# First modulations in two feature halves, and the first mixer's products in whole fp32

## The chip, the cores and the metric

The kernel runs on one core of one Trainium2 chip. The metric is the time on the device for one execution, in microseconds (us), as the median of several runs. TensorE (PE) does the matrix products, VectorE (DVE) and ScalarE (ACT) the elementwise work, GpSimd (POOL) issues some DMAs and does a little elementwise work, SyncE (SP) only issues DMAs. The engines run side by side and wait for each other on semaphores; each of them takes its own instructions strictly in the order of the program.

## The reference, cut to what matters

The input is x, 256 tokens of 1024 features, and a vector c. There are two layers of one model and two of a second one. All of it is fp32. What the change touches is the opening of the first layer:

```
c_act = silu(c)
mod   = (c_act @ mod_w[0] + mod_b[0])      # 1024 x 6144; six vectors of 1024
hin   = x * (1 + mod[1]) + mod[0]          # scale and shift, from the first 2048 columns
# first mixer (mla)
proj  = hin @ w_in                         # 1024 x (256 + 256 + 64): q rank, kv rank, rotary key
c_q   = rms_norm(proj[:, :256], q_norm);   c_kv = rms_norm(proj[:, 256:512], kv_norm)
k_r   = rope(proj[:, 512:])
q     = c_q @ w_uq                         # 256 x (8 heads x (128 + 64)), the 64 rotated
kv    = c_kv @ w_ukv                       # 256 x (8 heads x (128 + 128))
o     = causal softmax attention;  y = o @ w_o
x     = layer_norm(alpha * x + mod[2] * y);  then a gated convolutional ffn, and so on
```

## The kernel before, in words

The kernel is one hand-written program for each engine. Activations are kept transposed, features on the 128 partitions and the 256 tokens along the free dimension ("tiles(t, a, b)" is columns a*256 to b*256, one tile for 128 features).

**Weights.** All weight matrices come through one ordered list of chunks (weight_stream), each of up to 1 MB in two units. SP issues their DMAs into a ring of RAW = 3 chunks called raw. For each unit ACT writes a rounded copy to w_hi (L1058, in fp32r, the one-pass format of TensorE) and DVE the remainder, raw minus w_hi, to w_lo (L1575). Activations are split in the same way (h_hi and h_lo, o_hi and o_lo). A product is then three matmuls, hi x hi, lo x hi and hi x lo (L529 to L531 with the features as output, L535 to L537 with the tokens). ACT and DVE split AHEAD = 5 units in front of the product; "ahead(u)" issues the splits up to unit u and "product(key)" does this and then waits for the product's last matmul. SP refills a slot of raw when both units in it have been split.

**Modulations.** The vectors mod are sums over 8 row blocks of 128 rows (k = 0 to 7). They are not done on TensorE: for each row block, 128 x 2048 numbers are brought in, DVE multiplies them by c_act's column and adds them to modsum (L1602 for the first, L1605 for the others; this is modulate(count)). After eight of them, TensorE transposes modsum in blocks of 128 and DVE reduces over the columns (fold: L601 and L1623); coefficients() then writes scale and shift to lncol. Group 0 is the 2048 columns that hin needs; the 80 further row blocks of groups 1 to 10 are summed by DVE in gaps all through the program, fed by POOL's DMAs through the two slots of modraw, each refilled when the block two before has been summed. Of group 0 two blocks come through POOL into modraw, four through SP's queue (n in early, into the raw ring and into vv), two more through POOL.

**Opening, in order.** SP: c, the identity, the positions (broadcast, and once in a form of 4-byte pieces), the other constants, four blocks of group 0, x, small vectors, then the weights, of which the first three chunks (mla_in) wait until DVE has read the blocks of modulation in their slots. ACT: silu, then 17 DMAs of small parameter vectors into prow, which TensorE transposes (L783) and ACT copies to cols. TensorE: c, the parameters, x (L790), a small product for the relative bias (L796), the fold of group 0, then mla_in chunks 0, 1, 2. DVE: the eight sums of group 0 with the rotary angles between them, the fold, then for each of the 8 feature tiles hf (L1651) and h_lo (L1658), with ACT's h_hi (L1068). From mla_in the ranks go through squares, a sum by a matmul with ones (L813), a square root on ACT (L1311), reciprocal and scaling on DVE (L1955, L1958), a split into o_hi and o_lo (L1315, L1963); then uq(0), swap(0), ukv(0), uq(1), score of the first head and the attention loop, in which TensorE does ukv(1) at steps 0 and 1 and the first units of mla_o from step 4. DVE's part of a step begins with L1824 and ends with one modulate. Eight sums of groups 1 and 2 each: six are made before the attention loop, ten in it.

Of the kernel before, what the change touches and what calls it, by code (L numbers as in the profile page):

```python
# [16 lines left out]
P = 128  # L17
D = 1024
# [95 lines left out]
def weight_stream(w):  # L114
# [21 lines left out]
    cols(("mla_in", 0), mla_in, 0)  # L136
    cols(("mla_in", 1), mla_in, 256)
    cols(("mla_in", 2), mla_in, 512, 64)
# [43 lines left out]
def modulation_stream(w):  # L182
# [16 lines left out]
    for g in range(len(groups)):  # L199
        rows(g, groups[g])  # L200
    return out


def build(nc, w, consts, out):
# [5 lines left out]
    mods = modulation_stream(w)  # L210
# [8 lines left out]
    for n, (key, parts, _) in enumerate(chunks):  # L219
        count[n % RAW] += 16 * {"uq": 2, "wax": 1}.get(key[0], len(parts))  # L220
        landed.append(count[n % RAW])


    early = range(MODRAW, MODRAW + RAW + 1)
# [9 lines left out]
    with ExitStack() as ctx:  # L234
# [76 lines left out]
        ranks = kk[:, 8 * S:12 * S]  # L311
# [3 lines left out]
        mod_width = [max(sum(src.shape[1] for src, _ in parts) for h, _, parts in mods if h == g) for g in range(NG)]  # L315
# [49 lines left out]
        def unit_ap(ring, u):  # L365
            n = u // 2
            half_len = length[n] // 2
            return ring[:, (u % UNITS) * UL:(u % UNITS) * UL + half_len]
# [9 lines left out]
        def raw_unit(u):  # L378
            n = u // 2
            half_len = length[n] // 2  # L380
            return raw[:, n % RAW, (u % 2) * half_len:(u % 2 + 1) * half_len]
# [13 lines left out]

        beside_units = {
            "mla": {t: unit0("ukv", 1) + t for t in range(2)} | {t: unit0("mla_o", 0) + t - 4 for t in range(4, 9)},
# [9 lines left out]

        def early_slot(n):
            return raw[:, n - MODRAW, :] if n < MODRAW + RAW else vv[:, 0:2048]
# [5 lines left out]
        def _(sp):  # L415
            for i, name in enumerate(("c", "c_2")):
                sp.dma_start(prow[8 * i:8 * i + 8, 0:P],
                             w[name].rearrange("a (n q) -> (a n) q", q=P)).then_inc(sem("c_in"), 16)
            sp.dma_start(cst[:, C_ID:C_ID + P], consts[:, C_ID:C_ID + P]).then_inc(sem("ident_in"), 16)
            sp.dma_start(pos_i, w["positions"].broadcast_to([P, S])).then_inc(sem("pos_in"), 16)  # L420
            sp.dma_start(posq_i[:, :], w["positions"][0].rearrange("(t p) -> p t", p=P), allow_slow_non_contiguous=True).then_inc(sem("pos_in"), 16)
# [1136 lines left out]
        def _(dve):  # L1558
# [381 lines left out]
            for m in range(KT + 1):  # L1940
# [3 lines left out]
                if m:  # L1944
                    h_low(0, m - 1)
# [330 lines left out]
```

## Time and profile before

| | |
|---|---|
| median of 3 runs | 941.89 us (940.87 to 942.15) |
| the profiled execution | 945.47 us, span 943.7 us from the first to the last instruction |
| PE busy | 844.6 us, 90% of the span |
| DVE busy | 739.3 us, 78% |
| ACT busy | 526.4 us, 56% |
| DMA | 216.31 MB, mean 229 GB/s |
| first three-matmul product begins | 49.4 us into the span |
| first row maximum of the first attention (L1824) | 102.1 us |

[...]

### The profile page before, as it was taken

To read this page: it belongs to the slowest core of one execution; us is meant where nothing else is said; L and a number is where in the kernel's file an instruction comes from. 1 tells how busy PE (TensorE), PEld (TensorE's weight loads), DVE (VectorE), ACT (ScalarE), POOL (GpSimd) and SP (SyncE) were. 2 spreads that over 40 slices of the span, in tenths; PEclk is the share of its full clock that TensorE was granted. 3 is DMA by queue.
4 is the path that set the end of the run, shared out by engine and by line. 5 is a ranking of instruction groups with operands and counts; after the bars stand their busy time and mean duration, and the time that the engine had idled before them with its cause. 6 is when DMAs were issued, how large, how long until landed. Compare 5 with 4: busy or idle time off the path is not lost.

```text
span 943.7 us, 14975 instructions
## 1 busy us (share of the span) xinstructions
PE 844.6 (90%) x5749; PEld 776.7 (82%) x5749; DVE 739.3 (78%) x1153; ACT 526.4 (56%) x899; POOL 80.8 (9%) x118
## 2 busy tenths in 40 slices
PE   0386798999999998999999999999788999999886
PEld 0376677999999998999789999999677899879874
DVE  2879878878788778889878888676768866788886
ACT  0354665654444447449584345544474768766783
POOL 1000010002000000014000022010000000000120
PEclk9887989999999999999999999999989999999989
DMA  8966746577978864995956789987444784437431
GB/s 324 311 217 204 289 159 203 186 273 240 345 273 296 299 217 147 382 371 176 350 172 225 282 262 289 270 237 248 155 123 125 245 276 171 150 121 244 135 134 44
DMA packets 122678, 216.31 MB, mean 229 GB/s; under 512 B 12235, under 2 KB 97975, under 8 KB 115440
## 3 DMA queue, kind: packets, MB, share of 16 engines
q1 hardware_dynamic: 106828, 134.79, 42.9%
q0 software_dynamic: 12960, 72.46, 22.1%
q10 hardware_dynamic: 2820, 8.11, 2.6%
q8 instruction: 46, 0.75, 0.3%
q14 instruction: 24, 0.20, 0.1%
HBM read 214.18 MB, written 1.15 MB: 228 GB/s over the span
## 4 chain that ended last, share of the span: by engine, by line
PE 60%; DVE 21%; ACT 9%; DMA 5%; issue 4%; SPq 0%; DVEq 0%; ACTq 0%
PE bank L529 11%; PE bank L530 11%; PE bank L531 11%; PE bank L535 7%; PE bank L537 7%; PE bank L536 7%; DVE w_lo L1575 4%; DVE modsum L1605 3%; DMA raw<-in_mod_w 2%; DMA modraw<-in_mod_w 2%; ACT w_hi L1058 1%; ACT kk L1125 1%; PE bank L601 1%; PE bank L596 1%; PE bank L655 1%
## 5 line engine op out<-in xcount | busy, mean ns | idle before, releaser
L529 PE MATMUL bank<-h_hi,w_hi 128*128 128x256 f32 (+2 forms) x1184 | 341.7, 289 | 19.9 <-DVE h_lo L1728 9.2
L1575 DVE TENSOR_TENSOR w_lo<-raw,w_hi 128x1024 fp32r<-128x1024 f32 (+2 forms) x250 | 291.8, 1204 | 67.4 <-ACT w_hi L1058 66.9
L530 PE MATMUL bank<-h_lo,w_hi 128*128 128x256 f32 (+2 forms) x1184 | 337.3, 285 | 0.0
L531 PE MATMUL bank<-h_hi,w_lo 128*128 128x256 f32 (+2 forms) x1184 | 337.2, 285 | 0.0
L1058 ACT ACTIVATE w_hi<-raw 128x1024 fp32r<-128x1024 f32 (+2 forms) x250 | 249.2, 1028 | 81.3 <-PE bank L531 28.2
L529 PEld LDWEIGHTS bank<-h_hi,w_hi 128*128 128x128 f32 (+2 forms) x1184 | 228.3, 193 | 26.2 <-issue 21.5
L530 PEld LDWEIGHTS bank<-h_lo,w_hi 128*128 128x128 f32 (+2 forms) x1184 | 228.5, 193 | 1.4 <-issue 0.5
L531 PEld LDWEIGHTS bank<-h_hi,w_lo 128*128 128x128 f32 (+2 forms) x1184 | 228.2, 193 | 0.2
L535 PE MATMUL bank<-w_hi,o_hi 128*128 128x512 f32 x312 | 124.9, 400 | 0.6 <-issue 0.6
L537 PE MATMUL bank<-w_hi,o_lo 128*128 128x512 f32 x312 | 121.7, 390 | 0.0
L536 PE MATMUL bank<-w_lo,o_hi 128*128 128x512 f32 x312 | 121.7, 390 | 0.0
L1605 DVE SCALAR_TENSOR_TENSOR modsum<-modraw,small,modsum 128x2048 f32<-128x2048 f32 (+1 forms) x45 | 90.7, 2015 | 6.7 <-DMA modraw<-in_mod_w 4.1
L535 PEld LDWEIGHTS bank<-w_hi,o_hi 128*128 128x128 f32 x312 | 58.7, 188 | 13.4 <-issue 2.2
L537 PEld LDWEIGHTS bank<-w_hi,o_lo 128*128 128x128 f32 x312 | 58.6, 188 | 12.7
L536 PEld LDWEIGHTS bank<-w_lo,o_hi 128*128 128x128 f32 x312 | 58.8, 188 | 11.4 <-issue 0.5
L471 POOL DMA_DIRECT2D modraw<-in_mod_w x52 | 27.9, 536 | 382.3 <-DVE modsum L1605 134.0
L1250 ACT ACTIVATE kk<-kk 128x512 f32<-128x512 f32 x22 | 13.9, 632 | 72.3 <-DVE kk L1876 72.3
L471 POOL DMA_DIRECT2D modraw<-in_ada_w x32 | 17.4, 545 | 382.9 <-DVE modsum L1605 199.0
L1605 DVE SCALAR_TENSOR_TENSOR of<-modraw,small,of 128x2048 f32<-128x2048 f32 (+1 forms) x21 | 41.9, 1995 | 3.5 <-DMA modraw<-in_mod_w 1.2
L1256 ACT ACTIVATE o_hi<-kk 128x512 fp32r<-128x512 f32 x22 | 13.9, 632 | 45.9 <-DVE kk L1880 43.9
L1245 ACT ACTIVATE kk<-bank,cols 128x256 f32<-128x256 f32 x44 | 22.4, 559 | 28.8 <-PE bank L531 28.5
L608 PE MATMUL bank<-h_hi,o_hi 128*128 128x256 f32 x141 | 22.2, 309 | 7.0 <-DVE prob L1677 3.8
(274 smaller groups left out, 1151.5 us busy)
## 6 DMA issues: line engine op xcount, KB each, us to landing
raw<-in_ffn_w_in SPq DMA_DIRECT2D x88, 512.0 KB, 6.0
modraw<-in_mod_w POOLq DMA_DIRECT2D x36, 1024.0 KB, 6.4
raw<-in_ffn_w_out SPq DMA_DIRECT2D x44, 512.0 KB, 7.2
modraw<-in_ada_w POOLq DMA_DIRECT2D x16, 1024.0 KB, 5.4
raw<-in_attn_w_in SPq DMA_DIRECT2D x26, 512.0 KB, 5.3
raw<-in_moba_w_in SPq DMA_DIRECT2D x24, 512.0 KB, 8.6
modraw<-in_mod_w POOLq DMA_DIRECT2D x16, 512.0 KB, 4.7
modraw<-in_ada_w POOLq DMA_DIRECT2D x16, 512.0 KB, 4.8
```

What stands on the lines that cost most here:

```text
L471: pool.dma_start(modraw[:, slot, at:at + src.shape[1]], src).then_inc(sem(f"mod_in{slot}"), 16)
L529: pe.matmul(dst, cut(hi(u)), a_hi, start=first, stop=False, skip_group_check=True)
L530: pe.matmul(dst, cut(hi(u)), a_lo, start=False, stop=False, skip_group_check=True)
L531: return pe.matmul(dst, cut(lo(u)), a_hi, start=False, stop=last, skip_group_check=True)
L535: pe.matmul(dst, a_hi, cut(hi(u)), start=first, stop=False, skip_group_check=True)
L536: pe.matmul(dst, a_hi, cut(lo(u)), start=False, stop=False, skip_group_check=True)
L537: return pe.matmul(dst, a_lo, cut(hi(u)), start=False, stop=last, skip_group_check=True)
L608: pe.matmul(bank[0][:, 0:S], o_hi[:, 0:P], tiles(h_hi, 0, 1), start=True, stop=True, skip_group_check=True)
L1058: act.activation(hi(v), raw_unit(v), ACT.Copy).then_inc(sem("w_hi_ready"), 1)
L1245: act.activation(tiles(conv, s, s + 1), bank[0][:, t * S:(t + 1) * S], ACT.Identity, bias=cb[:, f:f + 1], scale=w2[:, 2 * FT + f:2 * FT + ...
L1575: dve.tensor_tensor(lo(v), raw_unit(v), hi(v).bitcast(F32), ALU.subtract).then_inc(sem("w_lo_ready"), 1)
L1605: ins = dve.scalar_tensor_tensor(acc, src, ck, acc, ALU.mult, ALU.add)
```

## The change

Five things are changed together.

1. Group 0 is summed in two feature halves. first_half[k] holds, of shift and scale, the features 0 to 511 of row block k (128 x 2 x 512 numbers in pieces of 2 KB); the other half is the new group 0 of the list. The first halves are brought in first, the even ones by SP and the odd ones by POOL (x goes between k = 1 and k = 3 on POOL), and summed, folded and used for four feature tiles before DVE sums the second halves. ACT alone writes hf (first_rows); h_hi and h_lo of this norm are gone.
2. The chunks of mla_in are cut differently: (q, kv) of rows 0 to 511, (rotary of rows 0 to 511, q of rows 512 to 1023), (rotary and kv of rows 512 to 1023), so that three units need only the first four feature tiles.
3. mla_in, uq and ukv are multiplied in whole fp32 directly from raw: one matmul in place of three. Their 14 units are not split by ACT and DVE any more (both begin at split0, the first unit of mla_o), and SP refills their slots when TensorE has used them (w_used). The ranks stay fp32, in vv, and are not split.
4. The splits of mla_o fall into the attention loop, one unit a step.
5. The order of the DMAs: positions, the columns of constants and the buckets go behind mla_in, the other constants behind two more chunks; ACT issues mod_b and the three blocks of PB[2] first. The cosine's angle is derived from the sine's.

```diff
+    by_half = mod[0].rearrange("(k p) c -> k p c", p=P)[:, :, 0:2048].rearrange("k p (n h c) -> k p n h c", n=2, h=2)
+            for k in (0, 2, 4, 6):
+                first_modulation(k)
+            weights(0)
+            weights(1, (0,))
+            for n in (0, 2, 4, 6):
+                sp.wait_ge(sem("first_summed"), max(n - 1, 5))
+                sp.dma_start(row_halves(early_slot(n)), mods[n][2][0][0]).then_inc(sem(f"mod_early{n}"), 16)
+            weights(1, (1,))
+            weights(2)
...
+                if 2 * (n - RAW) < split0:
+                    sp.wait_ge(sem("w_used"), 2 * (n - RAW) + 2)
+                else:
+                    sp.wait_ge(sem("w_lo_ready"), 2 * (n - RAW) + 2 - split0)
...
+            for k in (1, 3, 5, 7):
+                if k == 3:
+                    pool.dma_start(x[:, :].rearrange("p (t f) -> p t f", t=2),
+                                   w["x"][0].rearrange("(t p) f -> p t f", p=P)).then_inc(sem("x_in"), 16)
+                pool.dma_start(row_halves(first_slot(k)), first_half[k]).then_inc(sem(f"first_in{k}"), 16)
...
+            mla_unit(0, bank[0], 0)
+            mla_unit(1, bank[1], 0)
+            mla_unit(2, bank[2], 0, 64)
+            pe.wait_ge(sem("x_copied"), 4)
+            fold(0, (4, 5), (1, 3))
...
+            mla_unit(3, bank[0], 1)
+            mla_unit(4, bank[2], 1, 64)
+            pe.wait_ge(sem("bias_row"), 1)
+            rank_sum(0)
+            mla_unit(5, bank[1], 1)
+            rank_sum(1)
...
+                    for i in range(6):
+                        ins = pe.matmul(bank[5 + i // 2][:, (i % 2) * S:(i % 2 + 1) * S],
+                                        raw_unit(u)[:, i * P:(i + 1) * P], ranks[kt], start=kt == 0 and i % 2 == 0,
+                                        stop=kt == 1, skip_group_check=True)
...
             uq(0)
+            ukv_unit(0, 0)
             swap(0)
-            ukv_unit(0, 0)
             ukv_unit(0, 1)
             uq(1)
...
+            first_rows(0)
+            first_rows(1)
...
-            ahead(AHEAD)
-            for m in range(KT):
-                act.wait_ge(sem("h_full"), m + 1)
-                h_high(0, m, qz)
...
+            for k in range(KT):
+                acc, src = of_half(modsum[:, :], 0), row_halves(first_slot(k))
+                dve.wait_ge(sem(f"first_in{k}"), 16)
...
+            first_coefficients(0)
+            modulate(KT)
+            first_coefficients(1)
+            dve.wait_ge(sem("columns_in"), 16)
+            angles()
...
+            modulate(1)
+            rank_normed(0)
+            modulate(1)
+            rank_normed(1)
...
+            rotate(0)
+            modulate(3)
...
-            "mla": {t: unit0("ukv", 1) + t for t in range(2)} | {t: unit0("mla_o", 0) + t - 4 for t in range(4, 9)},
+            "mla": {t: split0 + t + 1 - AHEAD for t in range(-1, 9)},
```

## Rows read from the trace of the kernel before

**Rows 1.** Page, chain that ended last: shares by engine.

```profile
PE 60%; DVE 21%; ACT 9%; DMA 5%; issue 4%; SPq 0%; DVEq 0%; ACTq 0%
```

**Rows 2.** Busy time by stretch: PE, PEld, DVE, ACT, POOL, clock, DMA share, GB/s.

```profile
0.00:10.00 10.00, 0.28 (x1) 0.18 (x1) 1.41 (x3) 1.47 (x2) 2.74 (x9) 1.00 0.62 222
10.00:20.00 10.00, 0.00 (x0) 0.00 (x0) 4.19 (x2) 0.00 (x0) 0.53 (x1) 1.00 1.04 395
40.00:45.00 5.00, 3.79 (x16) 3.00 (x16) 3.13 (x4) 1.10 (x3) 0.53 (x1) 0.50 0.94 347
45.00:50.00 5.00, 0.65 (x4) 0.63 (x4) 4.25 (x11) 1.48 (x3) 0.00 (x0) 0.84 0.18 72
50.00:55.00 5.00, 4.86 (x23) 4.57 (x22) 4.53 (x12) 3.21 (x6) 0.00 (x0) 0.50 0.07 29
...
0.00:34.00 34.00, 3.72 (x17) 3.37 (x18) 16.95 (x21) 3.27 (x9) 3.27 (x10) 1.00 0.91 341
34.00:102.00 68.00, 49.69 (x303) 44.67 (x301) 57.59 (x76) 34.23 (x51) 4.30 (x8) 0.82 0.69 233
```

**Rows 3.** Timeline of 0 to 50 us: DVE's last sums, TensorE's fold, first product.

```profile
36.25 4.81 DVE L1605 SCALAR_TENSOR_TENSOR modsum<-modraw,small,modsum 128x2048 f32<-128x2048 f32 x2
41.21 3.84 PE L601 MATMUL bank<-cst,modsum 128*128 128x128 f32 x16 [5.13 <-DVE modsum L1605]
46.23 0.17 DVE L1645 COPY lncol<-modc 128x8 f32<-128x8 f32 x1
49.40 0.55 PE L529 MATMUL bank<-h_hi,w_hi 128*128 128x256 f32 x1 [4.35 <-DVE h_lo L1658]
```

**Rows 4.** Groups by line and form, 0 to 103 us: busy, mean ns, idle before.

```profile
L1575 DVE TENSOR_TENSOR w_lo<-raw,w_hi 128x1024 fp32r<-128x1024 f32 x11 | 13.1, 1220 | 1.1 <-ACT w_hi L1058 0.9
L1058 ACT ACTIVATE w_hi<-raw 128x1024 fp32r<-128x1024 f32 x11 | 11.2, 1056 | 5.9 <-PE bank L537 3.2 <-PE bank L531 2.2 <-DMA raw<-in_mla_w_ukv 0.5
L1068 ACT ACTIVATE h_hi<-qz,lncol 128x256 fp32r<-128x256 f32 x8 | 4.7, 598 | 8.1 <-DVE kk L1651 7.9
L1955 DVE RECIPROCAL rstd<-rstd 128x256 f32<-128x256 f32 x2 | 3.5, 1750 | 1.0 <-ACT rstd L1311 1.0
L1623 DVE TENSOR_REDUCE modc<-bank 128x4 f32<-128x512 f32 x4 | 2.8, 692 | 2.0 <-PE bank L601 2.0
L1958 DVE SCALAR_TENSOR_TENSOR kk<-bank,cols,rstd 128x256 f32<-128x256 f32 x4 | 1.8, 481 | 0.1
```

**Rows 5.** The same view, 102 to 150 us: sums over 1024 columns.

```profile
L1605 DVE SCALAR_TENSOR_TENSOR kk<-modraw,small,kk 128x1024 f32<-128x1024 f32 x7 | 9.0, 1280 | 4.3 <-DMA modraw<-in_mod_w 4.3
L1602 DVE TENSOR_SCALAR kk<-modraw,small 128x1024 f32<-128x1024 f32 x1 | 0.7, 745 | 0.0
```

**Rows 6.** Timeline of PE: spacing of split products, whole products, transposes.

```profile
51.25 0.41 PE L531 MATMUL bank<-h_hi,w_lo 128*128 128x256 f32 x1
51.46 0.41 PE L529 MATMUL bank<-h_hi,w_hi 128*128 128x256 f32 x1
...
57.12 0.28 PE L529 MATMUL bank<-h_hi,w_hi 128*128 128x256 f32 x1
57.24 0.28 PE L530 MATMUL bank<-h_lo,w_hi 128*128 128x256 f32 x1
...
97.31 0.59 PE L655 MATMUL bank<-of 128*128 128x256 f32 x2
97.75 0.38 PE L652 MATMUL bank<-kk,qz 128*128 128x128 f32 x2
```

**Rows 7.** Waits of 0 to 150 us, and DMA issues with median time to landing.

```profile
PE bank L783 <- DMA kk<-in_ffn_conv_b: 25.1, 1, 25.1
...
modraw<-in_mod_w POOLq DMA_DIRECT2D x12, 1024.0 KB, 5.9
```

**Rows 8.** Timeline of DVE about the first attention's start.

```profile
102.11 0.28 DVE L1824 CUSTOM_DVE_ANT_0 prob<-bank,cst 128x128 f32<-128x128 f32 x1
```

More of the change, by code:

```diff
@@ L209, in build @@
     length = [k * width for k, (_, _, width) in zip(row_tiles, chunks)]
-    mods = modulation_stream(w)
+    unit_len = [n // 2 for n in length for _ in range(2)]
+    paired = ("mla_in", "wax")
+    for n, (key, parts, _) in enumerate(chunks):
+        if key[0] in paired:
+            unit_len[2 * n:2 * n + 2] = [src.shape[1] * src.shape[2] for src, _ in parts]
+    mods, first_half = modulation_stream(w)
     NG = 1 + max(g for g, _, _ in mods)
@@ L219, in build @@
     for n, (key, parts, _) in enumerate(chunks):
-        count[n % RAW] += 16 * {"uq": 2, "wax": 1}.get(key[0], len(parts))
+        count[n % RAW] += 16 * {"uq": 2, "wax": 1, "mla_in": 1}.get(key[0], len(parts))
         landed.append(count[n % RAW])
-    early = range(MODRAW, MODRAW + RAW + 1)
+    early = range(KT)
     mod_slot = [n % MODRAW for n in range(len(mods))]
@@ L450, in _ @@
+            for i in range(2):
+                sp.dma_start(bf[8 * i:8 * i + 8, :], w["attn_b_f_2"].rearrange("a b -> b a"), allow_slow_non_contiguous=True).then_inc(
+                    sem("attn_in"), 16)
+            for n in range(RAW + 2, len(chunks)):
+                free_chunk(n)
+                weights(n)
             for t in range(2):
@@ L466, in modulation @@
                     slot = mod_slot[n]
[L467 to L469 removed]
+                    pool.wait_ge(sem("mod_summed"), {KT: 6, KT + 1: 8}.get(n, n - MODRAW + 1))
                     for src, at in mods[n][2]:
@@ L1283, in _ @@
                     at += n
+            for m in range(4):
+                act.wait_ge(sem("x_turned"), 2 * m + 2)
+                act.activation(tiles(qz, 2 * m, 2 * m + 2), bank[4 + m][:, :], ACT.Copy).then_inc(sem("x_copied"), 1)
             act.wait_ge(sem("params_turned"), 1)
@@ L1931, in _, with rank_normed @@
             link(dve.tensor_scalar(angle, pos, const(C_COL), None, ALU.mult))
-            modulate(1)
-            angles(sin, 0.0)
-            modulate(2)
-            angles(cos, 0.25)
-            modulate(2)
-            fold(0, (2, 0))
-            coefficients(0, mod8(0, 0), mod8(0, 1))
-            ahead(0)
-            for m in range(KT + 1):
-                if m < KT:
-                    dve.wait_ge(sem("x_copied"), m // 2 + 1)
-                    h_full(0, m, tiles(qz, m, m + 1))
-                if m:
-                    h_low(0, m - 1)
-            product("mla_in", 0)
-            modulate(1)
-            product("mla_in", 1)
-            for j in range(2):
-                if j:
-                    product("mla_in", 2)
+            angles()
+            def rank_normed(j):
                 dve.wait_ge(sem("c_rooted"), j + 1)
@@ L1982, in rotate @@
                                   ALU.add).then_inc(sem("q_rotated"), 1)
-            product("uq", 0)
             modulate(1)
-            rotate(0)
-            modulate(1)
-            product("ukv", 0)
+            dve.wait_ge(sem("const_in"), 16)
             causal = lambda t: (mask[:, 0:P], mask[:, P:CAUSAL])
```

317 lines of the change are left out of this document (170 added, 147 removed).

## The prediction

> **What bounds the kernel now.** I read the chain that ended last first: TensorE holds 60% of it, DVE 21%, DMA only 5% [rows 1]. So the kernel is TensorE-bound on the whole, but not in its opening. The busy times by stretch show that: up to 34 us TensorE works 3.7 us, up to 102 us another 50 of 68 [rows 2]. Before 34 us the DMA runs at 341 GB/s, after that at 233 [rows 2]. The timeline then gives the order of the opening: the eighth sum of group 0 ends at 41.06, the fold's transposes run 41.21 to 45.05, the coefficients are there at 46.4, the first product starts at 49.40 [rows 3], and the first attention's row maximum is at 102.11 [rows 8]. What follows 102 us is, but for small things, the same program in both kernels. So I work out when the changed kernel reaches that row maximum, and take what it gains there as the gain of the whole.
>
> **Step 1, first halves.** DMA has to bring 4 MB of first halves, 1 MB of x and 0.3 MB of the rest, and half of the 1.1 MB of weights behind the halves on SP gets in between: 5.85 MB. By 10 us 2.2 MB have moved (222 GB/s), then 0.395 MB a us [rows 2]: all is there at 10 + 3.65 / 0.395 = 19 us. A sum over 1024 columns is 1.28 us, the first of a group 0.75 [rows 5]; DVE needs 9.7 us for the eight and keeps up. They end at 20.3. A whole half-size pipeline could be as early as 18 or, if small pieces cost rate, 23. The parameters must be there too: now TensorE waits 25.1 us for the last of them [rows 7], to 29.4. I read that as small packets that take turns with 8 KB ones; against 2 KB ones they should be done by about 15. That is the least certain cover, and a rival below.
>
> **Step 2, to the first product.** Now 5.3 us pass from the last sum to the coefficients, with 16 transposes in 3.84 [rows 3]. Eight take 1.9, then one reduce of 0.69 [rows 4] and three small steps of 0.2: 3.4 us, so 23.7. One tile of hf on ACT is 0.6 (as the h_hi tile [rows 4]): TensorE starts at 24.3, not 49.4.
>
> **Step 3, whole products.** Split products of 256 columns start 0.21 us apart at the low clock and 0.12 at the high one; a whole product (two records) starts 0.43 before the next matmul at the high clock (97.31 to 97.75) [rows 6], so 0.86 at the low one. Three split ones are 0.36, so whole is dearer by 0.07 each. There are 40 in mla_in, 24 in uq, 32 equivalents in ukv: 96 x 0.07 = 7 us more of TensorE. Against that fall 14 units of splits, 1.22 us each at full width on DVE and 1.06 on ACT [rows 4], some 14 and 12 us with the shorter ones, all of which stand before the row maximum. [...]
>
> TensorE has been idle, so it starts low: at 49.4 it needed some 5 us before the spacing fell (clock 0.50 in 50 to 55 [rows 2]). First three units, 20 products: 6 at 0.86, 14 at 0.43, 11.2 us, to 35.5. Beside them DVE sums the second halves: 9.7 us from 23.7, to 33.4; their 4 MB (and rest of the weights) are there at 19 + 4.5 / 0.4 = 30.5, so DMA is hidden by 1.6 us. Second fold: eight transposes 1.0 at the high clock (half of the low price), reduce 0.7, small steps 0.9: 38.1, and hf on ACT to 38.7. Here TensorE is idle for some 2 us. If the clock falls there, the next 5 us run at half, 2.5 us lost. [...]
>
> **Step 4, ranks.** Units 3 and 4, 12 products: 5.2, to 43.9; sum with ones 0.86; unit 5, 3.4, to 48.2; square 0.6 and sum 0.9: 49.7. Root 0.4, reciprocal 1.75, two scalings of 0.48 [rows 4]: 52.8, then the rotary key's five small steps, 2.1: 54.9. The roots, reciprocals and angles for q are hidden under unit 5. TensorE's kr_spread waits for the constants, which now stand behind two chunks on SP; these go out after unit 3 (about 42), so they land near 51. uq(0) from 51.5, 12 x 0.43 = 5.2, to 56.7; ukv unit 0 (8 equivalents, 3.4) to 60.1; swap 0.9 to 61.0. Up to 1.3 us of constants are in this; each us later is a us on the path.
>
> **Step 5, DVE up to attention.** rotate(0), three passes of 0.7, to 63.1; then modulate(3), 2.4 each (two in 4.81 [rows 3]). The first two end at 67.9. The third waits: its slot of modraw is free when the first of them is summed (65.5), and landing takes 5.9 [rows 7], so 71.4, summed at 73.8. TensorE is done with the second ukv unit at 64.4 and with uq(1) at 69.6, and has scores at 71; it does not set the time. Row maximum at 73.8 instead of 102.1: 28.3 us earlier. Check by bytes: up to 102 us 34 x 0.341 + 68 x 0.233 = 27.4 MB moved [rows 2]; without the 2 MB of mla_o that may come later, 25.4 must be there by 71.4, a mean of 0.38 after the first 10 us, just under the 0.395 seen. So DMA is nearly the bound there; it can cost more, hardly give more.
>
> **Step 6, in attention.** DVE gets two more splits in the loop, ACT three (2.4 and 3.2 us, over ten steps), ukv(1) is 1.3 us longer, and TensorE no longer runs ahead of DVE at its start. What hides it: DVE's waits for modraw (4.3 us in this stretch [rows 5]) and ACT's slack. Nothing excludes that all 2.4 of DVE's splits show, nor that none does; I take 1.3. Everything later, the 64 sums of the later groups and all splits after mla_o's, is unchanged.
>
> **Sum.** 28.3 - 1.3 = 27 us. The span of 943.7 becomes 916.7, the profiled execution of 945.5 becomes 918.5. The median is 3.6 below that execution, 941.9: forecast 915.
>
> **Rivals.**
> - *The first half isn't early.* Parameters or first halves come as late as the parameters do now, 29.4 [rows 7]. The DMA share is 1.04 from 10 us on [rows 2], so they do compete; for me speaks that they are issued earlier and against smaller packets. 9 us of the 27 go: 924. Chance 14%.
> - *DMA paces the way to attention.* If it moves 0.35 MB a us instead of 0.395 after 10 us (pieces of 1 KB, slots freed late, a queue behind), 25.4 MB take until 76.3, and the two-slot stream then stays behind through its ten sums, some 4 more: 922. For it: the narrow byte check. Against: the sums in the loop have slack. 14%.
> - *Slower: TensorE stays at the low clock with whole products.* From 24.3: 17.2, fold and hf 4, then 10.3, 1.7, 6.9, 2.3, 1.7, uq 10.3, ukv 6.9, swap 1.7, 6.9, uq(1) 10.3, scores 2.6: 107 instead of 102, and ukv(1) of 13.8 us, where TensorE now runs ahead, 5 more: 952. It decides as soon as a whole product costs 0.8 us on average on this path. Against it: whole products of attention are at 0.43 [rows 6], and dense work always brought the high clock. 4%.
> - *More than forecast.* Halves at 17 us, no clock loss, TensorE ready first: 5 to 7 us more, 909. 8%.
> - *Forecast*, 915, with 910 to 920 as its own range: 60%.
>
> **How the numbers follow.** From no change to this kernel's measurement uncertainty is 0.2%, 1.9 us. All cases but one are faster; faster 0.94, same 0.02 (mixtures of the low clock and late data), slower 0.04. The range takes in both late cases and the early one: 907 to 926.
>
> **What would show it.** Right: first product near 24, the second stretch of products near 39, spacing 0.43 a product for most of them, uq starting before 53, row maximum of the first head at 74, then an attention loop of some 48 to 50 us as now, and the rest shifted. Wrong: a wait of TensorE for parameters after 20 us, long waits for modraw or raw between 50 and 80, a clock of 0.50 over several stretches, or the gain at the row maximum being lost again before the first layer norm.

## The result, and the profile after

The changed kernel takes 929.61 us (median of 4 runs, 928.32 to 931.48) against 941.68 (4 runs of the kernel before on the same chip): ratio 0.9864, 95% interval 0.983 to 0.9898. It is 12.1 us faster; 27 were forecast, and 929.6 lies above the range of 907 to 926. The profiled execution took 929.42, its span is 927.6.

The chain that ended last, shares by engine, answers to [rows 1]; then the busy time by stretch, columns as in [rows 2]:

```profile
PE 62%; DVE 17%; ACT 10%; DMA 6%; issue 4%; POOL 0%; DVEq 0%; ACTq 0%; POOLq 0%
```

```profile
0.00:10.00 10.00, 0.28 (x1) 0.18 (x1) 2.16 (x4) 1.67 (x3) 4.76 (x11) 1.00 0.76 253
10.00:20.00 10.00, 4.65 (x21) 4.09 (x21) 5.77 (x5) 2.39 (x4) 0.74 (x1) 1.00 1.05 376
...
40.00:45.00 5.00, 3.79 (x10) 3.08 (x11) 4.50 (x15) 4.04 (x7) 0.18 (x1) 0.66 1.14 354
...
50.00:55.00 5.00, 4.10 (x18) 2.96 (x16) 4.86 (x4) 0.97 (x3) 0.00 (x0) 1.00 0.95 339
...
0.00:34.00 34.00, 14.82 (x55) 12.35 (x56) 17.99 (x21) 6.96 (x16) 7.66 (x15) 1.00 0.97 338
34.00:102.00 68.00, 56.89 (x228) 41.80 (x227) 45.42 (x76) 25.02 (x52) 6.41 (x11) 0.91 0.80 269
```

VectorE's share of the chain fell from 21% to 17%, and TensorE now works 14.8 us of the first 34 instead of 3.7. But the clock is 0.66 from 40 to 45 us, and it falls once more, to 0.84 and then to 0.50 over a whole stretch:

```profile
55.00:60.00 5.00, 1.79 (x5) 0.98 (x5) 2.63 (x3) 2.31 (x4) 0.53 (x1) 0.84 1.02 317
60.00:65.00 5.00, 5.00 (x13) 4.01 (x13) 4.67 (x8) 0.00 (x0) 0.17 (x1) 0.50 0.63 233
```

At the start of this trace the clock column does not show how fast TensorE is: it reads 1.00 for the first 34 us, though the first 20 products take 11.45 us below and would take 8.6 at 0.43 each. There the spacing of starts is to be read, not the column.

The timeline of the kernel after, in order of time (start, length, engine, line); its rows answer to [rows 3] and [rows 8]:

```profile
19.37 2.67 DVE L1995 SCALAR_TENSOR_TENSOR modsum<-of,small,modsum 128x1024 f32<-128x1024 f32 x2 [1.04 <-DMA of<-in_mod_w]
...
26.19 11.45 PE L855 MATMUL bank<-kk,raw 128*128 128x256 f32 x40 [2.12 <-ACT kk L1362]
...
28.44 2.67 DVE L1678 SCALAR_TENSOR_TENSOR modsum<-modraw,small,modsum 128x1024 f32<-128x1024 f32 x2 [0.91 <-DMA modraw<-in_mod_w]
32.27 2.67 DVE L1678 SCALAR_TENSOR_TENSOR modsum<-modraw,small,modsum 128x1024 f32<-128x1024 f32 x2 [1.15 <-DMA modraw<-in_mod_w]
...
37.86 1.07 PE L651 MATMUL bank<-cst,modsum 128*128 128x128 f32 x8 [0.23 <-DVE modsum L1678]
...
41.21 7.25 PE L855 MATMUL bank<-kk,raw 128*128 128x256 f32 x24 [1.33 <-ACT kk L1362]
...
47.84 0.71 SPq L483 DMA_DIRECT2D cst<-in_constants  x1
...
53.66 1.13 PE L865 MATMUL bank<-kk,ones 128*128 128x256 f32 x4 [0.69 <-ACT kk L1374]
58.21 1.84 PE L892 MATMUL bank<-kk,cst 64*128 64x256 f32 x4 [3.42 <-issue]
59.98 8.04 PE L905 MATMUL bank<-vv,raw 128*128 128x256 f32 x24
...
72.36 0.69 DVE L2051 TENSOR_TENSOR kk<-of,bias 128x512 f32<-128x512 f32 x1 [5.79 <-PE bank L916]
...
74.42 4.81 DVE L1678 SCALAR_TENSOR_TENSOR modsum<-modraw,small,modsum 128x2048 f32<-128x2048 f32 x2
...
75.60 5.34 PE L905 MATMUL bank<-vv,raw 128*128 128x256 f32 x24
...
84.78 2.35 DVE L1678 SCALAR_TENSOR_TENSOR modsum<-modraw,small,modsum 128x2048 f32<-128x2048 f32 x1 [5.55 <-DMA modraw<-in_mod_w]
...
87.05 0.29 DVE L1886 CUSTOM_DVE_ANT_0 prob<-bank,cst 128x128 f32<-128x128 f32 x1
```

The reader is to see three things. (A whole product is two records, 40 for the 20 of the first three units, where each of the split ones in [rows 6] is one; L855 is mla_in, L892 kr_spread, the small product for the rotary key, and L905 uq. The durations recorded there overlap, 0.28 us with starts 0.12 apart, so a product's price is the spacing of starts.) The row maximum of the first head comes at 87.05, not at 73.8. The same 24 records (12 products) of L905 take 8.04 us at 59.98 and 5.34 at 75.60: that is the clock, 0.50 from 60 to 65 us and 1.00 from 75 to 80. And two gaps grew: 3.42 us before kr_spread (L892), which the view puts down to "issue", and 5.55 us of VectorE before its last sum. From the row maximum to the end it is 840.5 us, 841.6 before: what was gained stands at this point. The program has two waits before kr_spread, for the fold and for the constants, and the word "issue" names neither. The constants were issued at 47.84 and took 10.3 us to land, to 58.14, just before the 58.21; e1 below tests it.

Against the prediction's own steps, in us:

| step | forecast | after | late by | new at this step |
|---|---|---|---|---|
| first product | 24.3 | 26.19 | 1.9 | 1.9 |
| its 20 products end | 35.5 | 37.6 | 2.1 | 0.2 |
| second stretch of products | 38.7 | 41.2 | 2.5 | 0.4 |
| units 3 and 4 end | 43.9 | 48.4 | 4.5 | 2.0 |
| second sum with ones ends | 49.7 | 54.8 | 5.1 | 0.6 |
| uq(0) starts | 51.5 | 60.0 | 8.5 | 3.4 |
| uq(0) ends | 56.7 | 68.0 | 11.3 | 2.8 |
| rotate(0) ends | 63.1 | 74.4 | 11.3 | 0 |
| row maximum | 73.8 | 87.05 | 13.2 | 1.9 |

### The profile page after: what moved, and what is told of

Same layout as the page of the kernel before. It is cut to its first block, busy times and chain, and to the rows that moved or that the text cites. A ratio compares the mean times of both kernels' runs of the same rounds, so it can differ in the third digit from the quotient of the medians.

```text
span 927.6 us, 14747 instructions
## 1 busy us (share of the span) xinstructions
PE 854.4 (92%) x5661; PEld 777.5 (84%) x5661; DVE 718.8 (77%) x1124; ACT 514.1 (55%) x885; POOL 85.7 (9%) x123
## 3 DMA queue, kind: packets, MB, share of 16 engines
HBM read 214.18 MB, written 1.15 MB: 232 GB/s over the span
## 4 chain that ended last, share of the span: by engine, by line
PE 62%; DVE 17%; ACT 10%; DMA 6%; issue 4%; POOL 0%; DVEq 0%; ACTq 0%; POOLq 0%
PE bank L579 11%; PE bank L580 11%; PE bank L581 11%; PE bank L585 7%; PE bank L587 7%; PE bank L586 7%; DMA modraw<-in_mod_w 6%; DVE w_lo L1646 3%; DVE modsum L1678 3%; ACT w_hi L1127 2%; ACT kk L1189 1%; PE bank L705 1%; PE bank L855 1%; DVE kk L2238 1%; DVE x L1743 1%
## 5 line engine op out<-in xcount | busy, mean ns | idle before, releaser
L579 PE MATMUL bank<-h_hi,w_hi 128*128 128x256 f32 x1144 | 330.3, 289 | 15.6 <-DVE h_lo L1790 9.2
L1646 DVE TENSOR_TENSOR w_lo<-raw,w_hi 128x1024 fp32r<-128x1024 f32 (+1 forms) x236 | 278.1, 1215 | 64.2 <-ACT w_hi L1127 63.8
L580 PE MATMUL bank<-h_lo,w_hi 128*128 128x256 f32 x1144 | 326.2, 285 | 0.0
L581 PE MATMUL bank<-h_hi,w_lo 128*128 128x256 f32 x1144 | 326.0, 285 | 0.0
L1127 ACT ACTIVATE w_hi<-raw 128x1024 fp32r<-128x1024 f32 (+1 forms) x236 | 238.1, 1036 | 75.1 <-PE bank L581 29.2
L579 PEld LDWEIGHTS bank<-h_hi,w_hi 128*128 128x128 f32 x1144 | 220.9, 193 | 21.0 <-issue 15.2
L580 PEld LDWEIGHTS bank<-h_lo,w_hi 128*128 128x128 f32 x1144 | 221.1, 193 | 1.5 <-issue 0.5
L581 PEld LDWEIGHTS bank<-h_hi,w_lo 128*128 128x128 f32 x1144 | 220.8, 193 | 0.4
L585 PE MATMUL bank<-w_hi,o_hi 128*128 128x512 f32 x304 | 121.7, 400 | 1.5 <-DVE o_lo L2179 0.8
L585 PEld LDWEIGHTS bank<-w_hi,o_hi 128*128 128x128 f32 x304 | 57.2, 188 | 14.3 <-issue 3.3
L586 PEld LDWEIGHTS bank<-w_lo,o_hi 128*128 128x128 f32 x304 | 57.2, 188 | 11.3 <-issue 0.5
L1945 DVE TENSOR_TENSOR o_lo<-kk,o_hi 128x512 fp32r<-128x512 f32 x22 | 15.2, 692 | 16.7 <-ACT o_hi L1320 16.7
```

The source lines that it names most:

```text
L579: pe.matmul(dst, cut(hi(u)), a_hi, start=first, stop=False, skip_group_check=True)
L580: pe.matmul(dst, cut(hi(u)), a_lo, start=False, stop=False, skip_group_check=True)
L581: return pe.matmul(dst, cut(lo(u)), a_hi, start=False, stop=last, skip_group_check=True)
L585: pe.matmul(dst, a_hi, cut(hi(u)), start=first, stop=False, skip_group_check=True)
L586: pe.matmul(dst, a_hi, cut(lo(u)), start=False, stop=False, skip_group_check=True)
L1127: act.activation(hi(v), raw_unit(v), ACT.Copy).then_inc(sem("w_hi_ready"), 1)
```

## The experiments

The theory that I set out to test: three costs, in series, make the 13 us. The constants that kr_spread needs are issued behind two weight chunks; the clock falls in each gap of TensorE; and the two-slot stream of modulation rows has its sums in the wrong places, three of them in a row just ahead of the attention. All kernels below are the kernel after with the edit shown; "row maximum" is that of the first head in the profiled execution (one for each kernel, two for after and before). The runs stood on several chips, on which the median of the kernel before was 941.5 to 943.4 us; the ratio is taken on the same chip, so two medians of the table that lie 1 or 2 us apart are not told apart by them.

| run | median us | ratio to before, 95% | row maximum |
|---|---|---|---|
| after (again, e11) | 929.16 | 0.9864 (0.9842 to 0.9886) | 86.90 |
| e1 constants early | 924.61 | 0.9805 (0.9776 to 0.9833) | 79.41 |
| e2 sums forward | 928.02 | 0.9843 (0.9818 to 0.9868) | 85.93 |
| e3 both | 919.40 | 0.9754 (0.9726 to 0.9782) | 76.58 |
| e4 filler | 924.80 | 0.9804 (0.9777 to 0.9832) | 81.73 |
| e5 one stage | 934.18 | 0.9901 (0.9882 to 0.992) | 91.18 |
| e6 order2 | 918.40 | 0.9744 (0.9721 to 0.9767) | 75.31 |
| e7 order2, filler | 918.26 | 0.9726 (0.9703 to 0.975) | 74.24 |
| e8 x last | 927.39 | 0.9834 (0.9811 to 0.9858) | 86.01 |
| e9 weights held | 917.70 | 0.9742 (0.9719 to 0.9765) | 74.87 |
| e10 order2, one stage | 927.85 | 0.984 (0.9815 to 0.9865) | 84.32 |
| e13 halves on POOL | 916.74 | 0.972 (0.9696 to 0.9745) | 74.10 |

**e1.** The transfer of the constants is moved:

```diff
             sp.dma_start(prob[0:BUCKETS + 1, 0:2 * S],
                          consts[0:BUCKETS + 1, C_BUCKET:C_END]).then_inc(sem("buckets_in"), 16)
+            sp.dma_start(cst[:, P:C_COL], consts[:, P:C_COL]).then_inc(sem("const_in"), 16)
...
             for n in (RAW, RAW + 1):
                 free_chunk(n)
                 weights(n)
-            sp.dma_start(cst[:, P:C_COL], consts[:, P:C_COL]).then_inc(sem("const_in"), 16)
```

> The constants of the rotary key and the mask are issued on SP before the fourth weight chunk (near 34 us) instead of behind the fifth (47.8). Theory A (the wait for them and the low clock behind it cost the row maximum some 7 us): TensorE starts kr_spread near 55 instead of 58.2, at the high clock, uq(0) takes 5.2 to 5.5 us instead of 8.0, the row maximum of the first head comes at about 80 instead of 87.05, the median is 922 to 924. Theory B (the two-slot stream of modulation rows paces the opening, so that a faster TensorE only makes VectorE wait longer): uq(0) is as fast as in A, but the row maximum comes at 85 or later and the median is 927 or more. Theory C (data: an early transfer of 0.45 MB pushes the weights or second halves back): a new wait of 1 to 2 us ahead of 45 us and a median of 929 or more.

Measured 924.61, 5.0 us less than the kernel after. Its timeline:

```profile
26.31 10.58 PE L855 MATMUL bank<-kk,raw 128*128 128x256 f32 x40 [2.11 <-ACT kk L1362]
...
41.41 5.56 PE L855 MATMUL bank<-kk,raw 128*128 128x256 f32 x24 [1.32 <-ACT kk L1362]
...
53.23 1.13 PE L892 MATMUL bank<-kk,cst 64*128 64x256 f32 x4
54.29 5.45 PE L905 MATMUL bank<-vv,raw 128*128 128x256 f32 x24
...
77.14 2.35 DVE L1678 SCALAR_TENSOR_TENSOR modsum<-modraw,small,modsum 128x2048 f32<-128x2048 f32 x1 [5.16 <-DMA modraw<-in_mod_w]
79.41 0.28 DVE L1886 CUSTOM_DVE_ANT_0 prob<-bank,cst 128x128 f32<-128x128 f32 x1
```

The gap named "issue" is gone, so it was the wait for the constants, and uq(0) runs at the high clock (5.45 us, 1.00 in the column from 50 to 60). Of the 7.6 us at the row maximum 1.7 are not the edit's: units 3 and 4 took 5.56 us here, but 7.25 in e3 and e6, which have the same edit, and this execution (921.11) is the fastest of its five. The wait of 5.16 us for the stream stays. Theory A, with the median 0.6 above its range; B and C fall.

**e2.** Only the order of VectorE's sums of group 1:

```diff
-            modulate(1)
+            modulate(2)
             rank_normed(0)
             modulate(1)
             rank_normed(1)
...
             modulate(1)
             dve.wait_ge(sem("const_in"), 16)
...
+            modulate(1)
             rotate(0)
-            modulate(3)
+            modulate(1)
```

> The six sums of the second group that stand before the attention are moved on VectorE, nothing else: two instead of one before the first rank scaling, then one, then one behind the rotary key, one between distances and rotate(0), one behind it, instead of 1, 1, 1 and three behind rotate(0). They use the 4.2 us idle ahead of 50 us, the 2.5 ahead of 52.6 and the 5.8 ahead of rotate(0). Theory A (TensorE with its wait and clock sets rotate(0) at 72.4, the stream only the 5.5 us of wait behind it and two sums of 2.4): the row maximum comes as soon as scores are there, 81 to 82 instead of 87.05, median 924 to 925.5. Theory B (the stream alone is what is late): the same 5 us here, but then e1 brings nothing. Theory C (what is gained ahead of the attention is lost in it, because ring and slots are no further): row maximum at 82 and a median above 928.

Measured 928.02, 1.6 us less than the kernel after, whose runs it overlaps; 924 to 925.5 was expected. The theory was incomplete, and the timeline says why:

```profile
48.45 0.53 POOL L510 DMA_DIRECT2D modraw<-in_mod_w  x1 [2.33 <-DVE modsum L1678]
...
61.73 2.04 PE L892 MATMUL bank<-kk,cst 64*128 64x256 f32 x4 [7.42 <-issue]
...
78.06 2.35 DVE L1678 SCALAR_TENSOR_TENSOR modsum<-modraw,small,modsum 128x2048 f32<-128x2048 f32 x1
85.93 0.29 DVE L1886 CUSTOM_DVE_ANT_0 prob<-bank,cst 128x128 f32<-128x128 f32 x1 [5.53 <-PE bank L705]
```

The wait of VectorE for the stream ahead of its last sum is gone as foreseen. But a slot that is free earlier starts a transfer of 1 MB earlier (48.45; 55.19 in the kernel after), beside the constants. These take 14.3 us to land instead of 10.3, and kr_spread starts 3.5 us later still. The row maximum now waits for TensorE's scores. An earlier transfer took its time from the one that mattered.

**e3.** Both edits.

> e1 and e2 together. If TensorE's wait and clock and the stream of modulation rows are two costs in series, as theory A has it, they add up: row maximum of the first head at 74 to 77, median 916 to 920. If both only hide one another (theory B), the better of the two remains: row maximum at 80 or later, 922 or more.

Measured 919.40 and 76.58: theory A. Together they bring 10.2 us, apart 5.0 and 1.6, so that they do more than add up: e2 alone delays the constants, and e1 alone leaves the wait for the stream.

**e4.** Products that nobody reads, in TensorE's two gaps:

```diff
+            def filler(count, b):
+                for _ in range(count):
+                    pe.matmul(bank[b][:, 0:S], ones[:, :], tiles(hf, 0, 1), start=True, stop=True,
+                              skip_group_check=True)
...
+            filler(4, 6)
             mla_unit(3, bank[0], 1)
...
+            filler(8, 5)
             pe.wait_ge(sem("fold_summed"), 2)
             pe.wait_ge(sem("const_in"), 16)
```

> The kernel after with TensorE kept at work in its two gaps by products whose result nobody reads: four (1.7 us) after the second fold, eight (3.4 us) before the wait for the constants. Constants and order of sums are as in the kernel after, so that only the clock changes. Theory A (the low clock after each gap costs 2.0 and 3.8 us): units 3 and 4 take 5.3 us instead of 7.25, uq(0) 5.3 instead of 8.04, rotate(0) starts near 68.5 instead of 72.4, the row maximum is 3 to 4 us earlier and the median 925.5 to 927. If the clock falls whatever TensorE does there (power or another cause): spacing of 0.86 us stays, and the median is 929 or a little more by the fillers themselves.

Measured 924.80: 4.8 us for 5.6 us of useless work, and 0.7 more than the best that was expected. Its timeline:

```profile
25.95 11.59 PE L855 MATMUL bank<-kk,raw 128*128 128x256 f32 x40 [2.12 <-ACT kk L1369]
...
41.41 5.49 PE L855 MATMUL bank<-kk,raw 128*128 128x256 f32 x24
...
57.98 5.45 PE L912 MATMUL bank<-vv,raw 128*128 128x256 f32 x24
```

Every stretch from 40 to 80 us shows a clock of 1.00, and rotate(0) starts at 67.78. No other instruction was moved, so the low clock costs some 5 us, with the later constants that follow from it: 4.8 in the median, 5.3 at the row maximum (81.73).

**e5.** Second fold ahead of the first product:

```diff
+            pe.wait_ge(sem("x_copied"), 4)
+            fold(0, (4, 5), (1, 3))
             mla_unit(0, bank[0], 0)
             mla_unit(1, bank[1], 0)
             mla_unit(2, bank[2], 0, 64)
-            pe.wait_ge(sem("x_copied"), 4)
-            fold(0, (4, 5), (1, 3))
```

> The kernel after with the second fold put ahead of the first three product units on TensorE: the products start only when all sums are there, as if the group had one stage; whole products, transfers and the order of sums stay. Theory A (halves are worth the work that TensorE does before the second fold, 11.5 us less the two gaps with low clock): second fold near 37.3, first product near 39.5 instead of 26.2, 32 products in a row to 57, unit 4 done 8 to 9 us later than the 48.46 of the kernel after, the wait for the constants gone, row maximum at 93 to 96, median 935 to 938. Rival (the halves are worth nothing, what was gained came from whole products and from the order of the transfers alone; what follows is paced by the stream): row maximum at 87 to 89 and a median of 930 to 931.

Measured 934.18 and 91.18, both just under the ranges of theory A. The timeline of this kernel:

```profile
39.49 10.07 PE L855 MATMUL bank<-kk,raw 128*128 128x256 f32 x40
...
50.44 5.59 PE L855 MATMUL bank<-kk,raw 128*128 128x256 f32 x24
...
64.11 1.10 PE L892 MATMUL bank<-kk,cst 64*128 64x256 f32 x4 [1.74 <-issue]
65.13 7.13 PE L905 MATMUL bank<-vv,raw 128*128 128x256 f32 x24
```

TensorE starts 13.3 us later than in the kernel after and has lost only 4.1 by the row maximum: no gap after the fold, half of the wait for the constants, one low stretch fewer. So in the kernel after the halves are worth 3 to 4.6 us: 4.6 by the medians (934.2 less 929.6), 4.1 at the row maximum, and 2.9 if each gain is taken against the kernel before on its own chip (12.1 and 9.2). The other parts of the change, which e5 keeps, make the rest of the 12.1, some 7.5 to 9; how it divides between whole products and the order of transfers was not tried.

**e6.** As e3, third sum behind the rotary key:

```diff
-            modulate(1)
+            modulate(2)
             rank_normed(0)
-            modulate(1)
             rank_normed(1)
...
-            modulate(1)
+            modulate(2)
             dve.wait_ge(sem("const_in"), 16)
...
             rotate(0)
-            modulate(3)
+            modulate(2)
```

> As e3, but the third sum of the second group stands behind the rotary key instead of before the second rank scaling, since in e3 VectorE waited 2.7 us for its row there and held back the rotary key, for which TensorE then waited 1.24. Theory A: rotary key ready near 58 instead of 61.9, no wait of TensorE ahead of ukv, row maximum at 75.3 instead of 76.6, median 917.5 to 919.5. Rival: the stream is a sum behind again and the last sum before the attention ends at 78 or later; median 920 or more.

Measured 918.40 and 75.31, 1.3 earlier than e3 at the row maximum; the wait before ukv is gone. Theory A; in the medians 1.0 is within the runs' spread.

**e7.** e6 with `filler(4, 6)` as in e4.

> e6 with four products that nobody reads (1.7 us) in the gap after the second fold, as in e4. Theory A (the low clock after this gap of 1.3 to 1.5 us costs 1.7 us in units 3 and 4, whatever else is mended): these units take 5.5 us instead of 7.25, row maximum near 73.6, the time of the prediction, and a median of 915 to 917.5. Rival: with TensorE earlier, the rows of group 1 or the constants are late instead: the gain at unit 4 is 1.7 us, at the row maximum below 0.5, and the median that of e6.

```profile
37.72 1.06 PE L651 MATMUL bank<-cst,modsum 128*128 128x128 f32 x8 [0.86 <-DVE modsum L1684]
...
39.66 1.99 PE L871 MATMUL bank<-kk,ones 128*128 128x256 f32 x8
41.49 5.49 PE L855 MATMUL bank<-kk,raw 128*128 128x256 f32 x24
...
54.30 5.45 PE L911 MATMUL bank<-vv,raw 128*128 128x256 f32 x24
...
71.97 2.35 DVE L1684 SCALAR_TENSOR_TENSOR modsum<-modraw,small,modsum 128x2048 f32<-128x2048 f32 x1 [1.25 <-DMA modraw<-in_mod_w]
74.24 0.28 DVE L1892 CUSTOM_DVE_ANT_0 prob<-bank,cst 128x128 f32<-128x128 f32 x1
```

Row maximum 74.24, 0.4 from the forecast's 73.8. Of the 1.3 us that uq(0) starts earlier than in e6, 1.1 are left at the row maximum, since the stream now ends last again (1.25 at 71.97), and none is seen in the median, 918.26. Between the two readings written down beforehand: the short units are A's, the time is the rival's. That the filler made the units short is not shown here: the first three units took 10.80 us, and in e1 and e8, where they took 10.58 and 10.70, units 3 and 4 were short without any filler. Only e4, with 11.59, shows the filler at work.

**e10.** e6 with the second fold first, as in e5: what are the halves worth once the wait for the constants and the order of the sums are mended?

> As e6 with the second fold ahead of the first product, as in e5. Theory A (half of the worth of the halves was given back to the two gaps with low clock and to the wait for the constants, which one stage does not have): against e7 (no gap, constants early) the one stage now costs what it costs at unit 4, 55.97 less 46.91, some 9 us: row maximum at 82.5 to 84, median 926 to 928. Rival (the halves are worth 4 to 5 us, whatever stands behind them, since the stream or the data sets the row maximum): row maximum at 78 to 80, median 922 to 923.

Measured 927.85 and 84.32: 9.6 us slower than e7, 10.1 at the row maximum, and 10.2 slower than e9 below, which ran on the same chip. Theory A. The halves are worth some 10 us here, of which the kernel as changed kept 3 to 4.6.

**e8.** x behind all first halves on POOL.

```diff
             for k in (1, 3, 5, 7):
-                if k == 3:
-                    pool.dma_start(x[:, :].rearrange("p (t f) -> p t f", t=2),
-                                   w["x"][0].rearrange("(t p) f -> p t f", p=P)).then_inc(sem("x_in"), 16)
                 pool.dma_start(row_halves(first_slot(k)), first_half[k]).then_inc(sem(f"first_in{k}"), 16)
+            pool.dma_start(x[:, :].rearrange("p (t f) -> p t f", t=2),
+                           w["x"][0].rearrange("(t p) f -> p t f", p=P)).then_inc(sem("x_in"), 16)
```

> The kernel after with the 1 MB of x issued behind all first halves on POOL instead of behind the first of them. Theory A (the eight first sums wait 4.3 us for halves because 7 MB share the first 20 us): sums end at 19.5 to 20.3 instead of 22.04 and, if x is there by 15, the first product starts near 24.3 as predicted instead of 26.2; median at most 1 to 2 us better. Rival (x is then the late one: it lands near 19, its sixteen transposes of 3.7 us and the parameters' stand before the fold): sums at 20, but the first product at 27 to 28, median 930 to 931.

**e9.** e7 with the first weights held back on SP.

```diff
-            weights(0)
-            weights(1, (0,))
+            sp.wait_ge(sem("first_summed"), 3)
+            weights(0, (0,))
             for n in (0, 2, 4, 6):
...
-            weights(1, (1,))
+            weights(0, (1,))
+            weights(1)
             weights(2)
```

> As e7, but SP issues the first 0.5 MB of weights only after three first halves are summed and the next 0.5 MB behind the second halves, so that the first halves share the first 20 us with 0.7 MB less. Theory A (first halves are late by their share of the transfers, but TensorE and VectorE then meet a data bound on all of the first 38 us): the eight first sums end near 20.3 instead of 22, the first product starts near 24.5, and the second sums still end at 36.5 to 38; row maximum within 1 us of e7's 74.2, median 917 to 919.5. Rival (the 1.9 us late start is on the path): row maximum 1.5 to 2 us earlier, median 915 to 916.5. Second rival: the weights of unit 0 or 1 are now late, TensorE waits for them, median 920 or more.

**e13.** e7 with the first halves 1 to 6 on POOL, and 0, x and 7 on SP.

```diff
-            for k in (0, 2, 4, 6):
-                first_modulation(k)
+            first_modulation(0)
+            sp.dma_start(x[:, :].rearrange("p (t f) -> p t f", t=2),
+                         w["x"][0].rearrange("(t p) f -> p t f", p=P)).then_inc(sem("x_in"), 16)
+            first_modulation(7)
...
-            for k in (1, 3, 5, 7):
-                if k == 3:
...
+            for k in range(1, 7):
```

> As e7, but six of the eight first halves are issued on POOL and only the first and the last, with x between them, on SP (in e7 POOL has four and x, SP four). e8 and e9 showed that neither x nor the weights hold back the eighth sum: SP's fourth half landed 15.7 to 15.9 us after its issue in all three, while SP's queue moved 0.13 MB a us and POOL's 0.25. Theory A (the queue with a third of the rate has half of the data): by these rates POOL's six halves are there at 17.5, SP's share at 18.1, the eight sums end near 20.2 instead of 22.0, the first product starts near 24.3, the prediction's figure; at the row maximum 1 to 2 us earlier than e7's 74.2, unless the 12.5 MB of the first 38 us bound the second sums. Median 916 to 918.5. Rival (the total rate of some 0.38 MB a us alone sets the last landing, whatever queue): sums end at 21.5 to 22.2, first product at 25.8 or later, nothing changes.

These three ask why the first product is 1.9 us late. Measured were 927.39 for e8, 917.70 for e9 and 916.74 for e13. The sums of halves 6 and 7 in the timelines of e8, e9 and e13, one fence for each:

```profile
19.18 2.67 DVE L1994 SCALAR_TENSOR_TENSOR modsum<-of,small,modsum 128x1024 f32<-128x1024 f32 x2 [1.03 <-DMA of<-in_mod_w]
```

```profile
19.27 2.68 DVE L2002 SCALAR_TENSOR_TENSOR modsum<-of,small,modsum 128x1024 f32<-128x1024 f32 x2 [1.00 <-DMA of<-in_mod_w]
```

```profile
19.51 2.67 DVE L2000 SCALAR_TENSOR_TENSOR modsum<-of,small,modsum 128x1024 f32<-128x1024 f32 x2 [0.48 <-DMA of<-in_mod_w]
```

Half 6 lands at 19.2 to 19.5, as in the kernel after (19.37), whichever queue it is on and whatever is taken from before it. My theory of x's and the weights' share fell with e8 and e9, and the one of the unequal queues with e13. In e8 half 6 still came by SP's queue, which had the smaller rate; in e9 the weights had stood behind the halves on SP's queue anyway; in e13 POOL had six halves to move. The medians of e9 and e13 and the row maximum of e9 (74.87) lie where theory A had put them, but its eight sums were to end near 20.3 and 20.2 and ended at 21.9 and 22.2: these times came true without their mechanism. The packets of the trace, counted by queue, show POOL's at 0.25 MB a us and SP's at 0.13 while both have work, 0.38 together, and SP's at 0.35 as soon as POOL's is empty. By the sum, some 5.6 MB are through at 18 us in all orders: the rival of e13, a bound by all of the data. The forecast's own 19 us for the data was right to 0.4; what it had wrong is that two sums stand behind the last landing, not one. That is 1.3 of the 1.9. e9 shows a price too: TensorE waits 1.07 us for unit 1's weights, so its second stretch begins at 42.07 instead of 41.49. By the medians e7, e9 and e13 cannot be told apart.

The late first product is not alone on the path. In the kernel after the second fold starts at 37.86, 0.2 us behind the last of the first products and 0.1 behind the last of the second sums. In e1, e7, e8 and e13 the first products end up to 1 us earlier, the fold then waits 0.8 to 1.2 us for the sums (0.86 in the line of e7 above), and it starts at 37.6 to 38.1 all the same.

**e11 and e12.** The kernels after and before once more.

> The kernel after once more, timed on the chip of e9 and e10, with a second profile. If the profile read is typical: median 928 to 931, row maximum at 86 to 88, units 3 and 4 in 7.25 or 5.6 us and uq(0) in about 8. If its waits were chance, row maximum off by more than 2 us.

> The kernel before, a second profile. The first profiled execution took 945.47, 3.6 us above the median. If that was spread over the whole program, as the sum of the prediction took it: row maximum again at 102 and a span of 940 to 942. If it lay in the opening: row maximum near 98.5 to 100, and then the gain of the changed kernel at this point is 12 to 13 us, not 15.

The kernel after repeats itself: 929.16, row maximum 86.90, units 3 and 4 in 7.25, uq(0) in 7.92. The kernel before doesn't. Its second profiled execution took 939.6, span 937.8. It is a single run, 1.9 us below the median of 941.5, and reads

```profile
75.30 2.35 DVE L1605 SCALAR_TENSOR_TENSOR modsum<-modraw,small,modsum 128x2048 f32<-128x2048 f32 x1
...
82.94 1.13 PE L848 MATMUL bank<-of,cst 128*128 128x256 f32 x4 [1.67 <-ACT of L1334]
...
99.53 0.28 DVE L1824 CUSTOM_DVE_ANT_0 prob<-bank,cst 128x128 f32<-128x128 f32 x1
```

where the first had this sum at 76.55, this product at 85.51 and the row maximum at 102.11 [rows 8]: 1.3, 2.6 and 2.6 us later. Between the first two stands uq(0), in stretches with a clock of 0.50 and 0.74 there (75 to 80 and 80 to 85 us) and of 0.67 and 1.00 here. Behind the row maximum the two executions differ by another 3.3 us (841.6 and 838.3). Gain at this point: 12.5 us against this execution (99.5 less 87.0), 15.1 against the first; the medians differ by 12.1.

## Why the prediction was wrong

What held. The place of the gain: after the row maximum both kernels need 841 us, within 1. The prices: 0.43 us for a whole product at the high clock (12 of them from 75.60 to 80.78), 11.45 us for the first three units against 11.2. The cover of the parameters: they are there at 19.02, later than the 15 that was read for them, but 3 us ahead of the fold that needs them, so the first rival did not happen. That data run near their bound in the opening: 376 and 374 GB/s from 10 to 20 and 20 to 30 us, 361 in the mean from 10 to 38. Step 6: from the row maximum to the end 840.5 us, against 841.6 and 838.3 in two executions of the kernel before; a loss of 1.3 us in the loop can neither be seen nor ruled out.

What failed, step by step of the sum:

- **Steps 3 and 4, the clock, 5.5 us.** This is the largest term. The prediction named it ("if the clock falls there, the next 5 us run at half, 2.5 us lost") and then took nothing for it in the sum. At 0.50 it cost 2.0 us in units 3 and 4, 0.7 in kr_spread (1.77 us to the next product instead of e1's 1.06) and 2.8 in uq(0). e4 removes it with nothing else changed: 4.8 us. The second drop followed the wait for the constants, so that one late transfer cost twice. On the first drop: transposes and nothing else did not leave TensorE slow every time, for in e1 five of them at 18.54 take 0.65 us, 1.08 in the kernel after, and TensorE had done nothing for 14 us before them but 16 transposes, in 3.68 us. Of the seven executions here with this fold and a gap of 1.3 us behind it, five (after, e11, e2, e3, e6) ran units 3 and 4 in 7.25 us and two (e1, e8) in 5.56: not sure, but more often than not, and I should have charged it. The outcome went with how early the clock had risen in the first three units: they took 11.45 to 11.79 us in the five and 10.58 and 10.70 in the two. What sets that is not shown.
- **Step 4, the constants, 2.1 us, and the cause of 3.5 of the clock's.** "They land near 51": they landed near 58. Their chunk ahead waits for unit 3, which ended at some 46.5 instead of 42, its own start and clock being late; its issue took 1.2 us more, and the constants 10.3 us to land instead of 9. The wait was 3.4 us instead of 1.3. With 0.7 of clock and 0.6 by which kr_spread was taken too short this is the table's 3.4.
- **Step 1, one sum for two.** 1.3 of the 1.9 us at the first product; a term of 1.28 that had to be 2.67.
- **Step 3, the cover of the second halves.** Their sums were to end at 33.4 with data 1.6 us ahead. They started 1.7 us late and waited 0.91 and 1.15 us for data, and the last ended at 37.7. They end together with the first products, so that either alone holds the 2.5 us by which the second stretch is late, and the time of the first product would not have come back by itself (e1, e7, e8, e13).
- **Step 5, the stream.** Counted right in kind (third sum waits for its slot), but the slot was issued 0.3 us after it came free and landing took 7.7 us, not 5.9: the 1.9 us of the table, with 0.2 less in small steps.
- **The sum itself, 1.2 us.** The forecast took the 3.6 us by which the profiled execution of before lay above its median off the changed kernel too, and all of it behind the row maximum: 842.9 becomes 839.3 there, and 840.5 was measured, in an execution at its median. Part of the excess lay in the opening, which the forecast had replaced by worked-out times: of the 5.9 us between the two executions of before (spans of 943.7 and 937.8) 2.6 lie ahead of the row maximum. How much of the 3.6 that was is not known, since the second execution is not at the median either.

These make the difference: 13.2 us late at the row maximum and 1.2 behind it are 14.4 of the 14.6 us between 915 and 929.6. The rest is rounding.

The second rival (DMA paces the way to attention, 922) had the stream's slots right, and on the rate it was nearer than the forecast: 361 GB/s from 10 to 38 us against its 350 and the forecast's 395, and 268 from 38 to 85. But there the rate is no bound. Where it is low (129 GB/s from 45 to 50, 233 from 60 to 65), the queue waits for slots and chunks that TensorE and VectorE free late. e3 and e7 show it: with constants and sums mended the row maximum is at 76.6 and 74.2, e7 moves 336 GB/s from 38 to 72 us, and 916.7 to 919.4 us are reached by the same change. (By its own terms, 4.9 us to 76.3 and some 4 more, this rival comes to 924, not 922.) The forecast described, to within 2 to 4 us, the kernel that this one could have been; that e7's row maximum meets the forecast's to 0.4 us is partly luck, for its first product is as late as in the kernel after (26.06).

## What to carry to other kernels

When a change pulls a stage forward by tens of microseconds, list every transfer that the next stages wait for and date it by what stands before it on its queue, not by the data rate: here 0.45 MB of constants behind two chunks cost some 5 us, the wait and the low clock behind it. Price each gap of TensorE twice, once for itself and once for the slow stretch that may follow (here 2.0 us behind the first and 3.5 behind the second). And take the reference time for a gain worked out at one place from a second profile of the kernel before: two executions of one kernel differed by 2.6 us there and by 5.9 at the end.

## What the runs showed of the hardware

- A gap of TensorE of 1.3 us was followed by a fall of the clock to 0.50 (from 42 to 44 us) in five of seven executions (12 products in 7.25 us), and by none in two with the same instructions (5.56), in which the clock had risen earlier in the first products (10.58 and 10.70 us for 20 of them against 11.45 to 11.79). Products that nobody reads, put into the gap, went with 5.49 us for 12 in e4, whose first 20 took 11.59. e7, e9 and e13 show 5.49 too, but their clock rose as early as in e1 and e8, which kept it without filler (the clock column has 0.61 to 0.67 from 26 to 31 us in these five), so they prove little.
- Two queues with work did not share evenly in the kernel after: 0.25 MB a us for POOL's, 0.13 for SP's. From 8 to 10 us POOL's queue moved 124 packets with 0.51 MB and SP's 123 with 0.25 MB, as many packets and half the bytes. By their sum, 0.38, 5.6 MB were through at 18 us in after, e8, e9 and e13, and half 6 landed at 19.2 to 19.5 in all four, so that moving transfers between the queues gained nothing there.
- A slot freed earlier made another transfer later: in e2 the constants landed 3.5 us later because 1 MB of modulation rows started 6.7 us sooner.
